# Each weight block makes its three product terms in three passes, and waits for each remainder at its own term

## The reference

```python
for l in range(2):
    x = x + 0.5 * swiglu(rms_norm(x, g1[l]), w_gate[l], w_up[l], w_down[l])
    u = rms_norm(x, gm[l]) @ w_in[l]
    y_ssd, y_mla, y_conv = ...            # state space, attention, gated convolution
    x = x + concatenate([y_ssd, y_mla, y_conv]) @ w_out[l]
    x = x + 0.5 * swiglu(rms_norm(x, g2[l]), ...)
for l in range(2):
    proj = rms_norm(x, g[l]) @ w_in_2[l]
    ...                                   # differential attention ya, mLSTM yb
    x = x + (sigmoid(ga) * ya + sigmoid(gb) * yb) @ w_o[l]
```

## Time and profile before

| | |
|---|---|
| median of three runs | 1870.78 us (1869.59 to 1871.77) |
| the profiled execution | 1870.42 us |
| its span, first to last instruction | 1868.6 us |
| TensorE, matmuls | 1855.5 us busy, 9898 instructions |
| TensorE, weight loads | 1576.4 us busy |
| VectorE | 1219.2 us busy |
| ScalarE | 1069.4 us busy |
| GpSimd | 114.7 us busy |
| read from HBM | 307.16 MB |

### The profile page before, as it was taken

How to read it: one execution, slowest core, us unless ns; L and a number is a source line. 1 busy time by engine, 2 the same in 40 slices (tenths; PEclk the granted TensorE clock), 3 DMA queues, 4 the chain that set the end, 5 groups by cost and what they waited for, 6 DMA issues and landing times.

```text
span 1868.6 us, 25099 instructions
## 1 busy us (share of the span) xinstructions
PE 1855.5 (99%) x9898; PEld 1576.4 (84%) x9898; DVE 1219.2 (65%) x1798; ACT 1069.4 (57%) x1585; POOL 114.7 (6%) x91
## 2 busy tenths in 40 slices
PE   9999999999999999999999999999999999999999
PEld 7888998788888888899788888888888888888887
DVE  5655696775555555588776555597667478775745
ACT  6444677655444444476766444466776456667642
POOL 0000111100000000011200000002000000110000
PEclk9999999999999999999999999999999999999999
DMA  7555553245565555554235546554445555544563
GB/s 288 183 185 181 173 164 109 90 142 185 176 192 186 189 176 188 185 175 136 95 98 170 188 151 216 171 185 151 136 142 177 190 169 180 162 132 136 178 190 117
DMA packets 88886, 309.86 MB, mean 166 GB/s; under 512 B 9904, under 2 KB 10544, under 8 KB 88768
## 3 DMA queue, kind: packets, MB, share of 16 engines
q1 hardware_dynamic: 87984, 306.35, 50.4%
q0 software_dynamic: 496, 1.65, 0.2%
q10 hardware_dynamic: 288, 0.25, 0.0%
HBM read 307.16 MB, written 1.05 MB: 165 GB/s over the span
## 4 chain that ended last, share of the span: by engine, by line
PE 98%; DVE 1%; ACT 1%; issue 0%; POOL 0%; DVEq 0%; ACTq 0%
PE bank L1101 93%; PE bank L1098 4%; DVE WL L1947 0%; DVE XC L2096 0%; DVE MO L2266 0%; ACT MPT L1501 0%; DVE STATS L2257 0%; ACT MP L1501 0%; DVE X L2033 0%; ACT XS L1501 0%; DVE XDD L2303 0%; ACT QTK L1501 0%; DVE STATS L2254 0%; ACT ET L1501 0%; ACT QTQ L1501 0%
## 5 line engine op out<-in xcount | busy, mean ns | idle before, releaser
L1947 DVE TENSOR_TENSOR WL<-RAW,WH 128x1024 fp32r<-128x1024 f32 (+3 forms) x601 | 709.8, 1190 | 448.9 <-ACT WH L1501 444.7
L1501 ACT ACTIVATE WH<-RAW 128x1024 fp32r<-128x1024 f32 (+2 forms) x603 | 614.0, 1028 | 479.3 <-PE bank L1101 469.9
L1101 PE MATMUL bank<-WH,XTH 128*128 128x512 f32 (+2 forms) x1440 | 556.8, 387 | 0.9 <-DVE WL L1942 0.9
L1101 PE MATMUL bank<-WL,XTH 128*128 128x512 f32 (+2 forms) x1440 | 547.5, 380 | 0.0
L1101 PE MATMUL bank<-WH,XTL 128*128 128x512 f32 (+2 forms) x1440 | 546.9, 380 | 0.0
L1101 PE MATMUL bank<-WH,FR 128*128 128x512 f32 x1264 | 391.3, 391 | 0.0
L1101 PEld LDWEIGHTS bank<-WL,XTH 128*128 128x128 f32 x1440 | 270.9, 188 | 51.3
L1101 PEld LDWEIGHTS bank<-WH,XTH 128*128 128x128 f32 x1440 | 271.2, 188 | 50.7 <-issue 1.4
L1101 PEld LDWEIGHTS bank<-WH,XTL 128*128 128x128 f32 x1440 | 271.4, 188 | 49.5 <-issue 1.4
L1101 PEld LDWEIGHTS bank<-WH,FR 128*128 128x128 f32 x1264 | 234.0, 188 | 48.7
L1101 PE MATMUL bank<-WL,FR 128*128 128x512 f32 x632 | 247.8, 392 | 0.0
(11 more groups left out here) (316 smaller groups left out, 1639.6 us busy)
## 6 DMA issues: line engine op xcount, KB each, us to landing
RAW<-in_WALL_dram SPq DMA_DIRECT2D x553, 512.0 KB, 3.3
RAW<-in_WALL_dram SPq DMA_DIRECT2D x40, 256.0 KB, 2.6
RAW<-in_WALL_dram SPq DMA_DIRECT2D x8, 448.0 KB, 3.3
X<-in_x_dram SPq DMA_DIRECT2D x4, 256.0 KB, 5.2
out_dram<-X SPq DMA_DIRECT2D x4, 256.0 KB, 2.0
ROWP<-in_ROWP_dram POOLq DMA_DIRECT2D x1, 672.0 KB, 10.3
CONSTS<-in_CST_dram POOLq DMA_DIRECT2D x1, 664.0 KB, 7.9
ROUNDED<-in_CSTR_dram POOLq DMA_DIRECT2D x1, 208.0 KB, 12.5
```

The lines of the kernel that those rows point to most:

```text
L1101: return self.e.matmul(out, lhs, rhs, start=start, stop=stop, skip_group_check=True)
L1501: return self.e.activation(out, in_, func, **k)
L1947: self.e.tensor_tensor(lo, raw, hi.bitcast(F32), ALU.subtract).then_inc(*self.up("lo", j))
```

## The change

In a block, TensorE no longer makes the three terms of one chunk and half before it goes to the next. It makes the first term (xh·wh) for all chunks and halves, then the second (xl·wh), then the third (xh·wl). In a Lin's last block this is done for half 0 and then for half 1. It waits for `hi` of the weights at the block's start and for `lo` only ahead of the third pass, and for `left_hi` of a chunk in the first pass and `left` in the second. Block 0 makes the first two terms of each chunk, and the third terms at its end.

The planner's `start` follows this: a block may start when the high halves are there, a third of a block before the low half of its left operand, and two thirds of a block before the low half of its weights. And `late_x` is added behind block 1, not behind block 0.

```diff
@@ Order
+        self.hi_ends, self.halves = {j: 0 for j in range(NSPLIT)}, {}
...
             if step[0] == "A":
+                self.halves[phase] = since
...
+        self.hi_ends[j] = self.at["A"] + HOP["A"]
...
     def start(self, lin):
         n, when = len(lin.blocks), self.at["P"]
+        third = self.length(lin, n) // (6 if n == len(lin.parts) - 1 else 3)
         for c in lin.parts[n]:
...
-            when = max(when, self.ends[phase])
+            when = max(when, self.halves[phase], self.ends[phase] - third)
...
-        return max(when, self.split_ends.get(len(self.blocks), NEVER))
+        j = len(self.blocks)
+        return max(when, self.hi_ends.get(j, NEVER), self.split_ends.get(j, NEVER) - 2 * third)
...
-        if j == 0:
+        if j == 1:
             self.late_x()
@@ PE.block
-        w.wait_ge(*(self.at("lo", j) if j else self.at("lo_first", 0)))
-        if last and lin.kind != "thin":
...
+        if j == 0:
+            self.left_hi_made(lin.src, kk[0])
+            for n, c in chunks:
+                w.wait_ge(*(self.at("hi", 0) if n else self.at("hi_first", 0)))
+                for x in (0, 1):
+                    if x:
+                        self.left_made(lin.src, c)
+                    for half in range(2):
+                        self.products(lin, half, x, xh[:, c, :], xl[:, c, :], hi[:, n, :], lo[:, n, :], first and n == 0, False)
+            for n, c in chunks:
+                w.wait_ge(*(self.at("lo", 0) if n else self.at("lo_first", 0)))
+                for half in range(2):
+                    m = self.products(lin, half, 2, xh[:, c, :], xl[:, c, :], hi[:, n, :], lo[:, n, :], False, False)
             m.then_inc(*self.up("block", j))
+            return
+        w.wait_ge(*self.at("hi", j))
+        whole = last and lin.kind != "thin"
+        for halves in ((0,), (1,)) if whole else ((0,),) if lin.kind == "thin" else ((0, 1),):
+            for x in passes:
+                if x == 2:
+                    w.wait_ge(*self.at("lo", j))
+                for n, c in chunks:
+                    if x == 0:
+                        self.left_hi_made(lin.src, c)
+                    elif x == 1:
+                        self.left_made(lin.src, c)
+                    for half in halves:
+                        m = self.products(lin, half, x, xh[:, c, :], xl[:, c, :], hi[:, n, :], lo[:, n, :], first and n == 0,
+                                          last and n == len(kk) - 1)
+            if whole and halves == (0,):
+                m.then_inc(*self.up("half", lin.key))
+        m.then_inc(*self.up("block", j))
...
+    def left_hi_made(self, src, c):
+
+        name = src[0]
+        if name == "y" and c >= 12:
+            self.w.wait_ge(*self.at("cn_act", (src[1], "hi", c - 12)))
+            return
+        if name == "y":
+            name = "ys" if c < 8 else "mo"
+        self.w.wait_ge(*self.at("left_hi", (name, src[1], c // 2 * 2)))
@@ PE.products
+        left, right = (xl if x == 1 else xh), (lo if x == 2 else hi)
...
         if lin.kind == "tok":
-            o, s = ps[:, 0:lin.w], slice(128 * half, 128 * half + 128)
-            self.mm(o, xh[:, s], hi, st, False)
-            self.mm(o, xl[:, s], hi, False, False)
-            return self.mm(o, xh[:, s], lo, False, en)
+            return self.mm(ps[:, 0:lin.w], left[:, 128 * half:128 * half + 128], right, st, en)
...
         for f in range(2):
-            o, fs = ps[:, 256 * f:256 * f + 256], slice(256 * half + 128 * f, 256 * half + 128 * f + 128)
-            self.mm(o, hi[:, fs], xh, st and f == 0, False)
-            self.mm(o, hi[:, fs], xl, False, False)
-            m = self.mm(o, lo[:, fs], xh, False, en)
+            fs = slice(256 * half + 128 * f, 256 * half + 128 * f + 128)
+            m = self.mm(ps[:, 256 * f:256 * f + 256], right[:, fs], left, st and f == 0, en)
```

More of the change, by code:

```diff
@@ L280, in add @@
             since = self.at[step[0]] + HOP[step[0]]
+            if step[0] == "A":
+                self.halves[phase] = since
             if step[0] == "A":
@@ L419, in start, with length @@
             when = max(when, min(self.freed.get(p, 0) for p in free))
-        return max(when, self.split_ends.get(len(self.blocks), NEVER))
+        j = len(self.blocks)
+        return max(when, self.hi_ends.get(j, NEVER), self.split_ends.get(j, NEVER) - 2 * third)
+    def length(self, lin, n):
+        return max((272 if lin.kind == "tok" else 288) * len(lin.parts[n]) * lin.w // 1024, 60)
     def block(self, lin, when):
@@ L433, in block @@
         self.phases.append(("block", j))
-        self.at["P"] = when + max((272 if lin.kind == "tok" else 288) * size // 1024, 60)
+        self.at["P"] = when + self.length(lin, n)
         self.ends["block", j] = self.at["P"] + HOP["P"]
-        if j == 0:
+        if j == 1:
             self.late_x()
@@ L1122, in block @@
         xh, xl = k.left(lin.src[0])
-        w.wait_ge(*(self.at("lo", j) if j else self.at("lo_first", 0)))
-        if last and lin.kind != "thin":
[L1125 to L1138, removed]
-            m.then_inc(*self.up("block", j))
+        chunks = list(enumerate(kk))
@@ new lines, in block @@
+        passes = (0, 1, 2)
+        if j == 0:
[11 more added lines that the diff above has]
+                    m = self.products(lin, half, 2, xh[:, c, :], xl[:, c, :], hi[:, n, :], lo[:, n, :], False, False)
+            m.then_inc(*self.up("block", j))
+            return
@@ L1150, in left_made, with products @@
         self.w.wait_ge(*self.at("left", (name, src[1], c)))
-    def products(self, lin, half, xh, xl, hi, lo, st, en):
+    def products(self, lin, half, x, xh, xl, hi, lo, st, en):
         ps = self.k.PS[lin.pair[half]]
+        left, right = (xl if x == 1 else xh), (lo if x == 2 else hi)
+        st, en = st and x == 0, en and x == 2
         if st:
@@ L1157, in products @@
         if lin.kind == "tok":
-            o, s = ps[:, 0:lin.w], slice(128 * half, 128 * half + 128)
-            self.mm(o, xh[:, s], hi, st, False)
-            self.mm(o, xl[:, s], hi, False, False)
-            return self.mm(o, xh[:, s], lo, False, en)
+            return self.mm(ps[:, 0:lin.w], left[:, 128 * half:128 * half + 128], right, st, en)
         if lin.kind == "thin":
[L1163 to L1166, removed]
+            return self.mm(ps[0:16, 0:256], right, left, st, en)
         for f in range(2):
-            o, fs = ps[:, 256 * f:256 * f + 256], slice(256 * half + 128 * f, 256 * half + 128 * f + 128)
-            self.mm(o, hi[:, fs], xh, st and f == 0, False)
-            self.mm(o, hi[:, fs], xl, False, False)
-            m = self.mm(o, lo[:, fs], xh, False, en)
+            fs = slice(256 * half + 128 * f, 256 * half + 128 * f + 128)
+            m = self.mm(ps[:, 256 * f:256 * f + 256], right[:, fs], left, st and f == 0, en)
         return m
```

## The result

The changed kernel took 1880.23 us, the median of 7 runs (1876.02 to 1885.52). The kernel before took 1869.92 beside it (7 runs, 1869.59 to 1872.04). The ratio is 1.0052, with an interval of 1.0042 to 1.0061: slower by 10.3 us, where I had said 1872.8 with 1879.0 as the upper end. The profiled execution took 1885.06 and its span is 1883.3. The seven times stand in groups, at 1876 to 1877, at 1880 to 1881 and at 1885, and the granted clock of the whole run falls with them: 1.000 or 0.999, 0.997, 0.995.

The account below looks back on a forecast made before the run. TensorE's stream of matmuls was taken as the bound; pace 0, waits 0, start +0.38 and lost covers +1.86 gave +2.2 us, so 1872.8 us. Its own range was 1871 to 1876, over the cases 1867 to 1879.

Parts of the forecast that it names:

- The pace of the products: TensorE's matmuls in the reordered three passes: pace unchanged, taken as 0, bounds +7.3 and -3.6 us.
- rival 2: Products' pace changes with their new neighbours: up to 1880 or down to 1869.4; slower 10%, quicker 8%.
- The added waits: Waits in the middle of each block and for left_hi: semaphores long passed, cost 0, upper bound 0.11 us each.
- rival 1: Waits in the middle of blocks expose weight loads, 0.11 us each, 602 times: +66 us, 1937; 5%.
- The start: First blocks: block 0 gains 1.09 us, but block 2 stands 1.5 us behind the late flip; net +0.38 us.
- The four lost covers: Mix stages: wout 1 blocks no longer cover two flips of ys per stage; 2 x (0.24 + 0.69) = +1.86 us.
- the first flips of ys: First place in each mix stage where TensorE would stand for FR's rounded half: 0.24 us.
- the second place: Later flips of ys in each mix stage, where TensorE would stand for FR's rounded half: 0.69 us.
- the sentence on `start`: Planner: earlier block starts alter nothing where TensorE is the bound, so in all but the first few blocks.
- Rival 3: Plan runs apart at more than four places; the 3.7 us for MP may double or vanish: 1869 to 1877; 14%.
- The clock stays at 1.00: TensorE's granted clock over the whole run: no fall, since it held through 1.8 us of waiting for MP.

Follow-up runs that it names:

- E1: Changed kernel with the planner of before (old start(), late_x behind block 0), three passes and their waits kept: 1869.48 us, ratio 0.9994.
- E11: E1 with the lead of the finish chain in the mix stages at 104: 1878.90 us, ratio 1.0045.
- E9: Changed kernel with the list from block 112 to apply 9, in both mix stages, in the order of before, ScalarE's splits included: 1873.84 us, ratio 1.0015.
- E3: E1 with late_x behind block 1 (three passes, old start()): 1870.38 us, ratio 1.0000.
- E7: E3 with late_x adding split 2 ahead of both late flips, then split 3: 1869.59 us, ratio 0.9998.
- E4: Changed kernel with the lead of the finish chain in the mix stages at 98 instead of 100: 1873.22 us, ratio 1.0014.
- E10: Kernel before with only the lead of the finish chain in the mix stages at 104 instead of 100: 1877.06 us, ratio 1.0041.
- E5: Changed kernel with only blocks 113 and 309 and their splits moved back behind segment step 8: 1884.0 us, ratio 1.0075.
- E6: Changed kernel with 12 unused matmuls where TensorE waits for ET, ahead of apply 7 of each mix stage: 1877.37 us, ratio 1.0039.
- E8: Changed kernel run once more, unaltered, for its spread: 1880.70 us, ratio 1.0055.

## Why the prediction was wrong

*The pace of the products: right.* 0 was taken, and the pieces of 96 and 132 last 21.79 and 30.23 us in E1 for 21.78 and 30.22 before, so rival 2 is out. *The added waits: right*, and rival 1 (66 us) is out by the same run.

*The start: right, with some luck in the digits.* All the times came within 0.07 us, and the first full piece of 96 begins 0.39 us later than before (35.94 for 35.55), for a forecast of +0.38. But block 0 began anywhere between 7.25 us (E11) and 8.25 us (E1 and E9) in the other profiled executions with three passes. What is steady is the distance from block 0 to block 2: 8.03 us here and 8.05 in E3, for 8.09 forecast. E3, with the forecast start and the old order elsewhere, is +0.2 by the medians. E7 confirms the reason, split 2 behind the late flip.

*The four lost covers: right in E4, half right in the changed kernel.* The standing was 0.19 and 0.58 in E4 for 0.24 and 0.69 forecast, but a stage grew by 1.2 us for 0.93 forecast. Of the missing 0.4 between 0.77 and 1.2, two exposed loads at the 0.11 of the earlier trace rows would be about half; the rest I can't place. In the changed kernel itself the plan had already run apart. At the first flips of ys two `apply` steps stand behind them there instead of one, and TensorE does not wait; it stands only at the second place of each stage, 1.2 us in all for the 1.86 of the sum.

*The step that failed* is the sentence on `start`, "When TensorE is the planner's bound this alters nothing, which is so in all but the first few blocks: `when` there is at["P"]." Blocks 110 and 306, the first wout blocks behind the flips of mo, were bound by their left operand, by 5 units. I had looked for places where the comparison of `give` changes and had not looked for those where the start itself does. Against a margin of 4 units in the old plan, five units became a choice lost by one unit three blocks later. That took away a cover, and TensorE stood 1.64 us in each mix stage. E10 reproduces it with a lead alone, and E4, E5 and E9 narrow it: that one choice, and not block 113 alone but the order of three engines around it. Rival 3 named this course ("the plan runs apart further") with 14%, but its price, up to 1877, held only waits of the size seen before.

*The second failed step* is "The clock stays at 1.00: it held through 1.8 us of waiting for MP". It was an argument from one execution, and it doesn't hold for the wait for MP itself: in each of the profiled executions of E5 to E11 the clock fell behind it in one of the two stages, 1.7 us each time by the windows, though in none of those of before, the changed kernel and E1 to E4. Behind the wait for ET it fell for longer. The work on both sides of that wait is thin (19 matmuls with 2.36 us of work in the 4 us around it, none of them of a weight block); whether that makes the difference no run shows. E6 and E8 separate the price of the clock from that of the wait.

**The sum, remade.** Start +0.4. Per mix stage 2.8, measured as a whole in E8's undisturbed stage: 1.6 of it is the wait for ET (the 1.64 of the timeline), 0.9 is what E9 leaves (with the one wait for FR in it), and 0.3 I can't place. Twice that and the start is +6.0: 1869.9 + 6.0 = 1875.9; the lowest time is 1876.02. Each long stretch at half clock adds 4.4: 1880.3 with one and 1884.7 with both. The profiled execution has both and took 1885.06. The median, 1880.23, lies where one would put it, and the mean granted clock of those runs falls in the same steps; but it was not profiled, and a shorter stretch behind ET with one behind MP gives nearly the same (1.7 + 2.8 in E8).

What stays open: what makes the clock fall in one execution and not in the next, and for how long, with the same program. Smaller, a difference of 0.3 us between 104 and 139 us against before is for the most part one wait of 0.24 us for H of VectorE before 138.37, which E8, the same program, doesn't have.

## What to carry to other kernels

When a hand-written scheduler decides the order, a change of its figures is a change of the order everywhere. Diff the two orders it writes out before costing any instruction, since a rule "this changes nothing unless X binds" has to be checked at every block. A change whose whole worth is waits of 1.2 us can't pay for a reshuffled plan; here the passes with the old plan (E1) kept what there was to gain. Look for near ties: a choice won by 4 units out of 35000 fell the other way on an edit that meant something else, and where one side of it is 7 us worse, the margin belongs in the planner. And a cover is a property of all the queues around it: moving back one block with its split left the loss as it was or worse (E5, 1884.0), moving back the whole stretch took most of it away (E9, 1873.84).

## What was new of the hardware

A wait on TensorE has a second price. 1.6 us of standing among small products was followed by some 10.2 us at half of the clock in both stages of the first profile, 4.4 us lost for 1.6 waited. In other profiled executions the stretch was shorter (some 6.8 us in E8's first stage) or missing (E8's second stage). The Trainium skill (TensorE: Matmul & The Clock Gate, Part 1: The HAM clock gate) has TensorE at either 1.2 or 2.4 GHz, the lower of them when it has idled. The granted clock of 0.50 and 1.00 in these windows agrees. That the lower one follows TensorE's standing here is what E6 shows.

The kernel before seems to have it as well, smaller. On the chip of E8, its times lie at 1869.50 to 1870.52 (11) and at 1871.70 to 1872.30 (4). E7's profiled execution has the first stage of E3's order at 220.71 us instead of 219.03, and the windows behind the wait for MP read:

```profile
310.00:315.00 5.00, 3.29 (x14) 2.90 (x15) 1.95 (x5) 3.23 (x10) 0.32 (x1) 0.77 0.29 105
315.00:320.00 5.00, 5.00 (x25) 4.18 (x25) 1.56 (x3) 4.11 (x11) 0.00 (x0) 0.89 0.06 6
```

(0.23 + 0.11) x 5 = 1.7 us, which is what the stage is longer by, and about the distance of the two groups. That those slower runs of before are this same stretch is an inference; no execution of before with it was profiled.

A further wait in the middle of each of the 602 blocks, nearly all for events long passed, cost nothing that 11 runs or the length of a piece can tell (E1). And the order of the products, whether two neighbours share the weights or not, left each at 227.0 ns (21.79 us for 96).
